# A two-layer encoder step on one core: the last scatter written as token rows, and one subtraction moved ahead of the first convolution taps

## What is computed

```python
def _layer(x, ...):
    z = jnp.einsum('btd,dc->btc', x, w_in)      # rnn stream | q | k | v | two gates
    ...                                         # causal convolution (width 4), recurrence, banded attention
    x = _layernorm(DN_ALPHA * x + merged @ w_out, ln1_g, ln1_b)
    eidx, gate = _route(x2, w_router, e_bias)   # 8 of 64 experts for each token
    shared = (jax.nn.silu(x2 @ ws1) * (x2 @ ws3)) @ ws2
    ff = shared + _moe_routed(x2, eidx, gate, w1, w3, w2)
    x = _layernorm(DN_ALPHA * x + ff.reshape(B, T, D), ln2_g, ln2_b)
```

## Time and profile before

| | us |
|---|---|
| median of 3 runs | 1617.32 (1616.76 to 1618.33) |
| the profiled execution | 1616.29 |
| its span, first to last instruction | 1614.5 |
| PE busy in the span | 1567.4 (97%) |
| DVE busy | 746.6 (46%) |
| ACT busy | 570.8 (35%) |

### The profile page before, as it was taken

How to read it: one execution, slowest core, us unless ns; L and a number is a source line. 1 busy time by engine, 2 the same in 40 slices (tenths; PEclk the granted TensorE clock), 3 DMA queues, 4 the chain that set the end, 5 groups by cost and what they waited for, 6 DMA issues and landing times.

```text
span 1614.5 us, 25662 instructions
## 1 busy us (share of the span) xinstructions
PE 1567.4 (97%) x9488; PEld 1037.8 (64%) x9488; DVE 746.6 (46%) x1541; ACT 570.8 (35%) x1134; POOL 24.9 (2%) x40
## 2 busy tenths in 40 slices
PE   7999999999999999999999999999999999999995
PEld 6968997645555555545588699965555545455553
DVE  5668667234333323333574786562423333342336
ACT  4756433222232222223257664342223223222322
POOL 2000000000000000000010000000000000000000
PEclk9999999999999999999999999999999999999998
DMA  8552346499999999999436434458999999999990
GB/s 231 185 191 98 132 160 238 193 392 404 394 409 395 406 398 392 409 396 400 171 118 217 158 100 153 142 208 333 386 402 396 405 396 406 395 406 398 396 385 31
DMA packets 141556, 477.35 MB, mean 296 GB/s; under 512 B 10020, under 2 KB 74084, under 8 KB 108724
## 3 DMA queue, kind: packets, MB, share of 16 engines
q1 hardware_dynamic: 139728, 473.50, 75.9%
q0 software_dynamic: 1408, 2.85, 0.6%
q10 hardware_dynamic: 356, 0.13, 0.0%
HBM read 474.88 MB, written 1.57 MB: 295 GB/s over the span
## 4 chain that ended last, share of the span: by engine, by line
PE 92%; DVE 5%; ACT 1%; issue 1%; DMA 0%; SPq 0%; DVEq 0%; ACTq 0%
PE ps L911 27%; PE ps L931 14%; PE ps L562 6%; PE ps L575 6%; PE ps L576 6%; PE ps L577 6%; PE ps L952 4%; PE ps L893 4%; PE ps L953 4%; PE ps L894 4%; PE ps L896 2%; PE ps L940 1%; PE ps L872 1%; PE ps L919 1%; PE ps L696 1%
## 5 line engine op out<-in xcount | busy, mean ns | idle before, releaser
L911 PE MATMUL ps<-experts,xg 128*64 128x512 f32 x2048 | 450.5, 592 | 0.0
L911 PEld LDWEIGHTS ps<-experts,xg 128*64 128x64 f32 x2048 | 147.8, 137 | 290.6 <-issue 289.7
L931 PE MATMUL ps<-experts,hidT 128*64 128x512 f32 x1024 | 233.8, 598 | 1.0 <-ACT hidT L1276 1.0
L575 PE MATMUL ps<-parts 128*128 128x288 f32 x736 | 223.4, 304 | 2.4 <-DVE dense_lo L1404 2.1
L577 PE MATMUL ps<-parts,dense_lo 128*128 128x288 f32 x736 | 216.7, 294 | 0.0
L1730 DVE TENSOR_TENSOR hid<-ps,hid 128x256 f32<-128x256 f32 x64 | 27.2, 425 | 385.1 <-ACT hid L1270 385.1
L1284 ACT ACTIVATE yh<-ps,gsl 128x512 fp32r<-128x512 f32 x128 | 88.0, 687 | 229.9 <-PE ps L931 229.9
L1270 ACT ACTIVATE hid<-ps 128x256 f32<-128x256 f32 x64 | 24.6, 384 | 397.6 <-PE ps L911 397.6
L1262 ACT ACTIVATE xg<-ps,gperm_all 128x256 f32<-128x256 f32 x256 | 130.6, 561 | 63.0 <-PE ps L896 59.4
L1742 DVE SCALAR_TENSOR_TENSOR yl<-ps,gsl,yh 128x512 fp32r<-128x512 f32 x128 | 96.1, 751 | 122.8 <-ACT yh L1284 122.8
L931 PEld LDWEIGHTS ps<-experts,hidT 128*64 128x64 f32 x1024 | 68.2, 136 | 121.0 <-issue 121.0
(11 more groups left out here) (288 smaller groups left out, 2022.9 us busy)
## 6 DMA issues: line engine op xcount, KB each, us to landing
experts<-in_w SPq DMA_DIRECT2D x384, 1024.0 KB, 9.6
dense<-in_w_in SPq DMA_DIRECT2D x34, 1024.0 KB, 5.5
dense<-in_w_br_rnn SPq DMA_DIRECT2D x8, 1024.0 KB, 5.2
dense<-in_w_br_attn SPq DMA_DIRECT2D x8, 1024.0 KB, 5.2
dense<-in_w_out SPq DMA_DIRECT2D x8, 1024.0 KB, 5.2
dense<-in_ws SPq DMA_DIRECT2D x6, 1024.0 KB, 5.7
tok<-in_x_prompt SPq DMA_DIRECT2D x1, 1024.0 KB, 5.5
out_y_prompt<-tok SPq DMA_DIRECT2D x2, 512.0 KB, 2.6
```

The lines of the kernel that those rows point to most:

```text
L575: mm(bank[:, 0:T], w_hi[:, k, col:col + P], hi[:, k, :], start=k == 0, stop=False)
L911: last = mm(ps[e % 2 * CAP:(e % 2 + 1) * CAP, 2, :], xg[:, k, e * CAP:e * CAP + CAP], experts[:, e, 0:2, k * DE:k * DE + DE], start=k == 0 ...
L931: last = mm(ps[e % 2 * CAP:(e % 2 + 1) * CAP, 3 + b, :], hidT[:, m, e % 2 * CAP:(e % 2 + 1) * CAP], experts[:, e, 2, m * D + b * 512:m * D ...
```

## The change

In `combine_second`'s place PE now works per token tile t and feature half h. `kept_rows(t, h)` transposes four chunks of `ffT`, which at that time hold everything but the last half scatter, into one bank and leaves the accumulation open. `last_rows(t, h)` then adds two matmuls of 512 columns onto the same bank, with `ohT` (128 slots by the tokens of the tile) as the stationary operand and `yh` or `yl` as the moving one, so that tokens are the output rows. DVE's eight additions (`add_second`) are gone from the end of a layer. The banks of the token rows at this place change from (2, 3), (4, 5), (6, 7) to (0, 1), (5, 6), (2, 7), which leaves the two that `yl` is still read from, 3 and 4, untouched; the order of banks in the fill after it follows (`FILL`), and `keep_clock` works on bank 3. Apart from this, in the first layer alone, `low_parts` of piece 2 moves ahead of the first taps.

```diff
-FILL = tuple(range(KC))
+FILL = (tuple(range(KC)), (0, 1, 3, 4, 5, 6, 2, 7))
+ROWS = (((2, 3), (4, 5), (6, 7)), ((0, 1), (5, 6), (2, 7)))
...
-                combine_second(n)
-                to_tokens(ffT, lambda h: pe.wait_ge(c_added, FREE + n * KC + 4 * (h + 1)))
+
+                halves_kept = pe.snap(halves)
+
+                def kept_rows(t, h):
+                    at, m = TOK[t]
+                    for c in range(4 * h, 4 * h + 4):
+                        mm(ps[0:m, ROWS[1][t][h], c % 4 * P:c % 4 * P + P], ffT[:, c, at:at + m], ident,
+                           start=c % 4 == 0, stop=False, is_transpose=True)
+
+                def last_rows(t, h):
+                    at, m = TOK[t]
+                    pe.wait_ge(yl_ready, FREE + n * 4 + (3 + h))
+                    for part in (yh, yl):
+                        last = mm(ps[0:m, ROWS[1][t][h], :], ohT[:, 1, at:at + m], part[:, 1, 512 * h:512 * h + 512],
+                                  start=False, stop=part is yl)
+                    last.then_inc(tok_ps, 1)
+
+                pe.wait_ge(ohT_ready, FREE + n * 2 + 2)
+                pe.wait_ge(first_half_added, halves_kept)
+                kept_rows(0, 0)
+                kept_rows(0, 1)
+                last_rows(0, 0)
+                kept_rows(1, 0)
+                last_rows(0, 1)
+                kept_rows(1, 1)
+                last_rows(1, 0)
+                last_rows(1, 1)
+                for h in range(2):
+                    kept_rows(2, h)
+                for h in range(2):
+                    last_rows(2, h)
+                pe.sem_inc(c_full, KC)
                 pe.reg_add(done, done, 1)
                 if L < depth - 1:
-                    keep_clock(0, 3)
+                    keep_clock(3, 3)
...
                 for c in range(KC):
+                    if L == 0 and c == 0:
+                        low_parts(L, 1)
                     dve.wait_ge(first_tap, L * KC + c + 1)
...
-                    if c in (0, 3, 5, 7):
+                    if c in (0, 3, 5, 7) and (L, c) != (0, 0):
                         low_parts(L, (0, 3, 5, 7).index(c) + 1)
...
-                add_second(dve.snap(done))
                 dve.reg_add(done, done, 1)
-
                 stats(L, 1, LN_EPS)
+                dve.sem_inc(c_added, KC)
```

More of the change, by code:

```diff
@@ L599, in turned @@
                     for c in cs:
-                        last = transpose(ps[:, FILL[c], at:at + n], tok[0:n, t, c * P:c * P + P], ident[0:n, 0:n])
+                        last = transpose(ps[:, FILL[k][c], at:at + n], tok[0:n, t, c * P:c * P + P], ident[0:n, 0:n])
                         if t == NT - 1:
@@ L618, in fill_normed, with turn_chunk @@
                         turned(t, (c,))
-            def turn_chunk(src, t, c):
+            def turn_chunk(src, k, t, c):
                 at, n = TOK[t]
[L622 to L632, removed]
+                return transpose(ps[0:n, ROWS[k][t][c // 4], c % 4 * P:c % 4 * P + P], src[:, c, at:at + n], ident)
             def keep_clock(bank, n):
@@ L820, in _ @@
                             for c in range(4):
-                                last = turn_chunk(yP, t, c)
+                                last = turn_chunk(yP, 0, t, c)
                             last.then_inc(tok_ps, 1)
@@ L1059, in _ @@
                 act.wait_ge(z_ready[0], c // 2 + 1)
-                activation(xT[:, c, :], ps[:, FILL[c], 0:T], ACT.Copy).then_inc(z_free[0], 1)
+                activation(xT[:, c, :], ps[:, FILL[0][c], 0:T], ACT.Copy).then_inc(z_free[0], 1)
             def high_parts(L, f):
@@ L1084, in norm_rows, with norm_back @@
                     h = 0 if t < NT - 1 else 1
-                    activation(tok[0:n, t, 512 * h:D].rearrange("p (h c) -> p h c", c=512), ps[0:n, 2 + 2 * t + h:4 + 2 * t, :],
+                    a, b = ROWS[k][t][h], ROWS[k][t][1] + 1
+                    activation(tok[0:n, t, 512 * h:D].rearrange("p (h c) -> p h c", c=512), ps[0:n, a:b, :],
                                ACT.Identity, bias=mv[0:n, t, 0:1], scale=mv[0:n, t, 1:2]).then_inc(tok_act, 1)
-            def norm_back(L, g, b, first):
+            def norm_back(L, k, g, b, first):
                 for c in range(0, KC, 2):
                     act.wait_ge(z_ready[0], z_count(L, first + c) + 1)
-                    bank = ps[:, FILL[c], :]
+                    bank = ps[:, FILL[k][c], :]
                     activation(xT[:, c, :], bank[:, 0:T], ACT.Identity, bias=prm_all[:, L, b * KC + c:b * KC + c + 1],
@@ L1320, in _ @@
                 if L < depth - 1:
[L1321 removed]
+                    norm_back(L, 1, V_G2, V_B2, Z_FILL2)
         @block.vector
@@ L1447, in stats, with norm_back @@
                 dve.wait_ge(norm_set, (2 * L + k + 1) * NT)
-                V.tensor_scalar(tok[0:n, t, 0:512], ps[0:n, 2 + 2 * t, :], mv[0:n, t, 1:2], mv[0:n, t, 0:1],
+                V.tensor_scalar(tok[0:n, t, 0:512], ps[0:n, ROWS[k][t][0], :], mv[0:n, t, 1:2], mv[0:n, t, 0:1],
                                 ALU.mult, ALU.add).then_inc(tok_dve, 1)
-            def norm_back(L, g, b, first):
+            def norm_back(L, k, g, b, first):
                 for c in range(1, KC, 2):
                     dve.wait_ge(z_ready[1], z_count(L, first + c) + 1)
-                    bank = ps[:, FILL[c], :]
+                    bank = ps[:, FILL[k][c], :]
                     V.tensor_scalar(xT[:, c, :], bank[:, 0:T], prm_all[:, L, g * KC + c:g * KC + c + 1],
```

14 lines of the change are left out of this document (7 added, 7 removed).

## The result

The changed kernel takes 1608.46 us (median of 5), the kernel before, run beside it, 1618.33; the ratio is 0.9942 with a 95% interval of 0.9926 to 0.9958. That is faster by 0.58%; forecast were 1608.1 and 0.57%, range 1607.0 to 1611.6. One of the five runs of the changed kernel was disturbed (9060.86 us); it is left out of the ratio but stands in the median, which is 1608.34 without it.

What follows compares the result with a forecast made beforehand. PE, busy 97% of the span, was taken as the bound, so its waits had to shrink. Terms 1.95 + 3.65 + 3.65 = 9.25 us gave 1617.32 - 9.25 = 1608.1 us, 0.57% less; 8-in-10 range 1607.0 to 1611.6.

Steps and rivals of the forecast that it cites:

- The early low parts: First layer's start: low parts of piece 2 ahead of three taps remove a PE wait, 1.95 us gained.
- The end of a layer: Both layer ends: DVE's moments start directly behind the second yl, without its eight additions, 3.65 us gained at each.
- the start of the first transposes: Layer 1's end: eight transposes start at 1592.45, some 0.2 us before down's end, and lie under yl's second half.
- the end of the second bank: Layer 1's end: the second bank's last matmul, waiting for the second yl, ends at 1594.87.
- The transposes' pitch of 0.107: Layer ends: each PE transpose takes 0.107 us, from 20 in 2.40 with the last one's latency of 0.27.
- The rule of the Trainium skill: Layer ends: about 275 ns per transpose; as a pitch, about 2.3 us gained at each place, not 3.65.
- The bank is ready before DVE is free: Layer 1's end: first bank's second matmul ends at 1593.95, before DVE is free at 1594.15.
- The two covers at the boundary: After layer 0: ACT's table load hides 0.65 us behind tile 1's moments; keep_clock leaves 0.5 us before tile 1's fill.
- Absorption of the head: Rival, between 60 us and the experts: the first layer's 1.95 us is lost, 1610.0; chance 0.09.
- Dear wide matmuls: Rival, layer ends: 512-column fp32r matmuls cost 0.43 us each, total gain 5.7, time 1611.6; chance 0.06.
- No effect: Rival, layer ends: transposes don't run under yl, only the first layer's 1.95 us is left, 1615.4; chance 0.03.
- The fallen clock: Rival, layer boundary: 1.2 GHz for line 562 and the work behind it loses 14.4 us, time 1622.5; chance 0.03.

Runs made afterwards that it cites:

- e1: Kernel before with only the low parts of piece 2 moved ahead of the first taps; 1615.21 us against 1618.71, ratio 0.9984.
- e2: Changed kernel with the low parts back behind the first taps, so only the layer ends changed; 1610.48 us, ratio 0.9957.
- e8: Changed kernel without the branch and code for further rounds of experts on PE, ACT and DVE; 1607.73 us, ratio 0.9941.
- e6: Changed kernel with five matmuls in keep_clock instead of three; 1610.22 us, ratio 0.9952.
- e5: Changed kernel without keep_clock after layer 0; 1612.01 us, ratio 0.9966.
- e9: Changed kernel with a warm start: ten unread identity matmuls on PE while it waits for the input; 1610.12 us, ratio 0.9956.
- e10: Kernel of e9 with the bank-by-bank PE order of e4 at the layers' ends; 1608.85 us, ratio 0.995.
- e4: Changed kernel with PE's transposes and matmuls of one bank together, bank by bank; 1607.75 us, ratio 0.9939.
- e7: Changed kernel with 40 more semaphore instructions on PE during its input wait, moving its later code; 1610.54 us, ratio 0.9955.

## Why the prediction was right

**The early low parts, 1.95: right**, 1.98 in e1 and in the changed kernel. The steps are in the rows: the subtraction starts with the high parts, the taps follow without a gap, PE's one wait left there is 0.4, for piece 3 (0.35 before).

**The end of a layer, 3.65 each: right in mechanism, too large.** It measured 3.38 and 2.96 (e2: 3.14 and 2.93). The term that was mis-sized is the start of the first transposes.
- The prediction has "Eight transposes start behind `down`'s last matmul, which gives its place to the next some 0.2 before its end": 1592.45, 0.18 ahead of `down`'s end. They start 0.06 behind its end in layer 0 and 0.48 behind it in layer 1, so 0.24 and 0.66 late; the ends fell short by 0.27 and 0.69. Without the branch (e8) they start 0.07 ahead of `down`'s end, 0.11 late, and the ends are 3.48 shorter in both layers (14.26 - 10.78, 17.48 - 14.00), short by 0.17. The kernel before may have had the same issue time, hidden under its wait for `yl`; no row shows it.
- The way from there to the end of the second bank was right: 1590.23 to 1592.26 + 0.40 is 2.43, and the prediction's 1592.45 to 1594.87 is 2.42. Within it small errors cancel. The first of a pair behind transposes takes 0.32 up to the next start (1591.05 to 1591.37), 0.09 more than taken, twice on this way; against it the twelve transposes take 0.11 less than taken, and the 0.07 of waiting for `yl` was not needed. Otherwise the matmuls of 512 columns are pitched 0.23 (800.03 to 800.26 in layer 0's timeline) and end 0.39 to 0.40 after their start, as taken (0.225, 0.40).
- The transposes' pitch of 0.107 was good: eight take 0.82. The rule of the Trainium skill that was weighed there ("TensorE: Matmul & The Clock Gate", Part 4, about 275 ns each) agrees as a duration, 273 ns on average in this trace, and would be wrong as a pitch by a factor of 2.6. What the prediction made of it was also off: four more transposes stand ahead of the second bank, so by its own steps that pitch gives 1.8 us for each place and not 2.3.

The step "The bank is ready before DVE is free" failed with the first of these: in layer 1 DVE waits 0.52. PE's later banks were all in time.

**The two covers at the boundary: right.** `keep_clock` had 0.40 of room (0.5 read), shown by e6. ACT's table load held nothing up: its first root is done by 801.04 (0.19 from 800.85), and DVE's inverse takes it at 802.24, behind the moments of tile 1 and without a wait.

**The rivals.** Absorption of the head: excluded by e1. Dear wide matmuls: 0.23, not 0.43. No effect: excluded. The fallen clock: absent in the change (1.00 in every stretch of the boundary), and e5 shows what it would have cost, 3.05 and not the 14.4 that I had reckoned. That sum let the low level last through more than 14 us of work; it lasted 6.8 (803.97 to 810.80). The prediction gave for the clock of line 562, but they end at 801.00; that line's clock is known from its pace and from the trace's clock list. The Trainium skill's remark on the same page ("TensorE: Matmul & The Clock Gate", Part 4) that transposes don't count for the clock gate as other matmuls do fits e5, but e5 doesn't separate the transposes from the gaps. The start speaks against it: in the kernel before PE had done nothing but transposes, from 7.56 on, when the clock was up at 10.57.

**The total.** The parts give 8.43 where 9.25 was forecast: the two ends 0.96 too large, the head 0.03 too small, and 0.11 that nobody forecast in the stretch between, whose cause stays open. The medians' difference of 9.9 is larger than either. What lies behind the first table transpose is 1596.72 in the profiled run of before (1616.29 - 19.57) and 1588.28 in that of the changed kernel (1610.44 - 22.16). If it was so in all runs, an estimate, the medians had starts of 21.6 and 20.2, both within the range of the traces, and the difference of 1.4 is the excess. So the forecast median lay 0.4 from the measured one by luck: a gain forecast 0.8 too large met a start that was shorter by chance.

## What to carry to other kernels

Where a sum ends a stage, look at which operand is late and put everything that doesn't need it ahead of it on the same accumulator; here transposes of the part that was ready, and then only the two matmuls with the late part. When an engine's wait is removed, what had been hidden in it can come out: here an issue time of up to 0.6 us, or in e9 a transfer. To compare traces of a kernel whose start varies, cut them at events on both sides of the change; the head of the eight kernels with the early low parts and no warm start then agrees to 0.06 us where whole runs scatter by 3. And read a clock of 1.00 together with the pace of like instructions, at the start above all.

## What the runs showed of the hardware

- **The clock at the start.** The first projection of the same 32 instructions takes 8.00 to 8.03 in the traces of before, e2, e5, e8, e9 and e10, and 9.68 to 10.44 in the others. Its matmuls start 0.48 apart ahead of the moment at which the trace's clock list begins and 0.24 apart behind it. That moment lies between 8.61 and 17.66 in the twelve traces, at 10.57 in the kernel before; in the six with the short projection it lies ahead of the projection, in the others inside it. So the long start is the clock's lower level, 1.2 GHz, and the views' 1.00 ahead of that moment is not a measurement. PE's first matmul comes at 7.21 to 8.80 in the ten kernels without the warm start, and the clock is up 3.0 to 9.5 us later; what decides between these isn't shown.
- **The clock between two layers.** Gaps of 1.53 and 1.26 us around four short transposes were enough for 1.2 GHz (e5). A single gap amid other work was not: 0.40 in the changed kernel, 1.57 and 1.75 in the kernel before, 1.9 in e9.
- **The issue time behind a skipped branch**, as the profile's rows give it, was 0.20 to 0.60 in layer 0 of e2, e4, e6, e7, e9 and e10 and not listed in that of the changed kernel and e5; in layer 1 it was 0.18 to 0.50, and not listed in e9 and e10. Without the branch PE starts 0.13 earlier than in the best of these. What sets its length stays open: it varied with the same PE code (changed kernel and e2) and when the code was moved (e7). Nor is it shown that the old kernel had it, since its wait for `yl` would cover it.
